# Weighing in column halves with turned blocks of inverses, and part of the keys on GpSimd

## The reference, cut to what matters

```python
# mixer A: 8 heads of 64; a 64-token chunk sees itself and the 8 chunks before, with a bias by distance
sc = jnp.einsum('bqhd,bkhd->bhqk', qc, kc) * scale + bias
p = jax.nn.softmax(sc, axis=-1)
o = jnp.einsum('bhqk,bkhd->bqhd', p, vc)
# mixer B: 8 query heads on 2 key heads, a chunk sees itself and the one before, with one sink per head
m = jnp.maximum(jnp.max(sc, axis=-1, keepdims=True), sink)
p = jnp.exp(sc - m)
p = p / (jnp.sum(p, axis=-1, keepdims=True) + jnp.exp(sink - m))
o = jnp.einsum('bnhgqk,bnkhd->bnqhgd', p, vb)
```

## Time and profile before

| | us |
|---|---|
| median of 3 runs | 2675.07 (2673.93 to 2676.16) |
| the profiled execution | 2678.14 |
| its span | 2676.2 |
| TensorE busy | 2631.9 (98%) |
| attention stage, first layer | 238.2 |
| attention stage, second layer | 237.5 |

### The profile page before, as it was taken

The page is one execution under the profiler, slowest core; times in us unless marked ns, Lnnn a source line. Parts: engine busy times, 40 slices in busy tenths (PEclk is TensorE's granted clock), DMA queues, the critical chain, the costliest instruction groups (busy, mean ns, idle before and its releaser), DMA issues. The chain is left out here.

```text
span 2676.2 us, 36725 instructions
## 1 busy us (share of the span) xinstructions
PE 2631.9 (98%) x12920; PEld 2208.2 (83%) x12920; DVE 1923.2 (72%) x3579; ACT 1159.0 (43%) x2429; POOL 252.6 (9%) x390
## 2 busy tenths in 40 slices
PE   8999999999999999999999999999999999999998
PEld 6888888888888888888878888888888888888886
DVE  8766667644787787767996666775448887776687
ACT  6222677732533333344542227775325333333444
POOL 0000311244100000000000011112440000000000
PEclk9999999999999999999999999999999999999999
DMA  4323433253222332385423243332531332234843
GB/s 147 122 104 115 155 102 111 75 183 115 87 99 103 114 118 84 106 269 176 153 99 122 99 144 123 119 97 88 188 120 61 114 110 88 103 114 136 267 124 126
DMA packets 185236, 333.21 MB, mean 125 GB/s; under 512 B 17248, under 2 KB 62688, under 8 KB 185056
## 3 DMA queue, kind: packets, MB, share of 16 engines
q1 hardware_dynamic: 176832, 307.67, 34.6%
q10 hardware_dynamic: 8224, 23.20, 2.6%
HBM read 237.09 MB, written 92.80 MB: 123 GB/s over the span
## 5 line engine op out<-in xcount | busy, mean ns | idle before, releaser
L1203 PE MATMUL ps<-op_hi,up_hi 128*128 128x512 f32 x1232 | 479.9, 390 | 2.5 <-DVE third_sum L2781 2.5
L1205 PE MATMUL ps<-op_hi,up_lo 128*128 128x512 f32 x1232 | 479.3, 389 | 0.0
L1204 PE MATMUL ps<-op_lo,up_hi 128*128 128x512 f32 x1232 | 479.3, 389 | 0.0
L1203 PE MATMUL ps<-in_hi,up_hi 128*128 128x512 f32 x728 | 286.9, 394 | 3.3 <-DVE up_lo L2279 2.1
L1205 PE MATMUL ps<-in_hi,up_lo 128*128 128x512 f32 x728 | 285.0, 392 | 0.0
L1204 PE MATMUL ps<-in_lo,up_hi 128*128 128x512 f32 x728 | 285.0, 392 | 0.0
L1878 ACT ACTIVATE up_hi<-up_raw 128x512 fp32r<-128x512 f32 x252 | 158.0, 630 | 276.9 <-PE ps L1205 271.1
L1203 PEld LDWEIGHTS ps<-op_hi,up_hi 128*128 128x128 f32 x1232 | 231.3, 188 | 51.1 <-issue 3.3
L1205 PEld LDWEIGHTS ps<-op_hi,up_lo 128*128 128x128 f32 x1232 | 231.3, 188 | 48.3
L1204 PEld LDWEIGHTS ps<-op_lo,up_hi 128*128 128x128 f32 x1232 | 231.3, 188 | 47.6
L1173 POOL CAST w_hi<-w_raw 128x256 fp32r<-128x256 f32 x192 | 85.3, 486 | 1757.7 <-DMA w_raw<-w_lin 1199.7
(11 more groups left out here) (266 smaller groups left out, 5406.8 us busy)
## 6 DMA issues: line engine op xcount, KB each, us to landing
up_raw<-w_gu SPq DMA_DIRECT2D x42, 1024.0 KB, 5.1
act_raw<-ff_saved SPq DMA_DIRECT2D x154, 256.0 KB, 2.7
w_quarter<-w_lin SPq DMA_DIRECT2D x52, 512.0 KB, 4.4
w_raw<-w_lin SPq DMA_DIRECT2D x48, 512.0 KB, 3.7
ff_saved<-ff_block SPq DMA_DIRECT2D x88, 256.0 KB, 2.0
ff_saved<-ff_mix SPq DMA_DIRECT2D x66, 256.0 KB, 2.1
gated<-gates_saved SPq DMA_DIRECT2D x32, 512.0 KB, 4.1
stage<-in_saved SPq DMA_DIRECT2D x48, 256.0 KB, 2.8
```

The source lines that it names most:

```text
L1203: pe.matmul(out, w1, x1, start=first, stop=False, skip_group_check=True)
L1204: pe.matmul(out, w1, x0, start=False, stop=False, skip_group_check=True)
L1205: return pe.matmul(out, w0, x1, start=False, stop=last, skip_group_check=True)
```

## The change

1. `weigh` takes two units (one pair) at once, in even steps. Stationary are now 64 columns of values (one head), moving are 128 columns of turned probabilities. Head 0 writes PSUM rows 0 to 63, head 1 rows 64 to 127, in turn for each block of keys. The built program gives these matmuls a tile of 128x64 of the array at column 0 or column 64; all other matmuls have the tile 128x128. The result comes out with head dimensions in rows, as `x_sb` wants it.
2. The inverses must then lie along the columns. `invert_pair` writes them spread over 2x64 columns (`wide`, 128x128 in place of 128x2), TensorE turns that block (`turn_wide`, where `turn_pair` was), ScalarE copies it to the place of the result in `x_sb` (`take_wide`), and `take_heads` multiplies the weighed values by it there.
3. In mixer B the two units of a pair are turned in the same step and copied out of PSUM by one instruction of 256 columns in place of two of 128. There are three buffers `probs_t`, and the probabilities of B use both halves of two of the `probs` buffers, so that six units have their own place.
4. The splitting of 14 of the 16 key halves of a layer goes from ScalarE and VectorE to GpSimd (`split_keys`), which also does its weight splits in single parts of 128x256 at fixed steps (`split_parts`) so that keys come between them.
5. `FILL_A` puts the gate products of A mostly into steps without weighing (26 in A0 and 8 in each later A phase, as before). `vb_odd` lies in two pieces, so one more DMA shifts values.

The core of the diff:

```diff
-FILL_A = ((3, 3, 3, 2, 2, 2, 2, 1, 1, 1, 1, 1, 1, 1, 1, 1), (1, 1, 1, 1, 1, 0, 1, 0, 1, 0, 0, 0, 1, 0, 0, 0))
+FILL_A = ((3, 3, 3, 3, 2, 3, 1, 2, 1, 1, 0, 1, 1, 1, 0, 1), (0, 1, 0, 2, 0, 1, 0, 1, 0, 1, 0, 1, 0, 1, 0, 0))
...
+            def split_keys(L, c):
+
+                kind, _, half = CONV[c]
+                e, cols = KEYS.index(kind), slice(half * HALF, (half + 1) * HALF)
+                made, value = plain_when(L, c)
+                pool.wait_ge(*staged_when(L, c))
+                pool.tensor_copy(ka_hi[e][:, cols], staged(c)).then_inc(made, 1)
+                pool.wait_ge(made, value - 1)
+                pool.tensor_tensor(ka_lo[e][:, cols], staged(c), ka_hi[e][:, cols], ALU.subtract).then_inc(made, 1)
...
             for L in range(DEPTH):
-                for t in range(TILES):
+                split(L, 0)
+                split(L, 1)
+                for s in range(UNITS):
+                    for c in conv_at(s, *KEYS):
+                        split_keys(L, c)
+                    for t, part in split_parts(s):
+                        split_part(L, t, part)
+                for t in range(GATE_TILES, TILES):
                     split(L, t)
...
-                pe.wait_ge(turned_ready, L * UNITS + u + 1)
-                n = L * (UNITS // 2) + u // 2
+                pe.wait_ge(turned_ready, L * TURN_GROUPS + groups_turned(u))
                 taken = n - 1 if mixer == "B" and u % PHASE > 1 else n
-                if e == 0 and taken > 0:
+                if taken > 0:
                     pe.wait_ge(head_free, taken)
                 for j in range(nb):
-                    mm = pe.matmul(o_ps(u)[:, e * HD:(e + 1) * HD], probs_t[u % 2][:, j * P:(j + 1) * P], values[j],
-                                   start=(j == 0), stop=(j == nb - 1))
+                    for e in range(2):
+                        rows = slice(e * HD, (e + 1) * HD)
+                        mm = pe.matmul(o_ps(u)[rows, :], blocks[j][:, rows], turns[e][:, j * P:(j + 1) * P],
+                                       start=(j == 0), stop=(j == nb - 1))
                 mm.then_inc(head_done, 1)
 
-            def turn_pair(L, u):
-
-                n = L * (UNITS // 2) + u // 2
-                pe.wait_ge(head_free, n + 1)
+            def turn_wide(L, s, u):
+
+                n = L * HEAD_PAIRS + u // 2
+                pe.wait_ge(inverse_ready, n + 1)
                 if n > 0:
-                    pe.wait_ge(pair_ready, n)
-                pe.transpose(p_ps, o_tok[:, n % 2, :], ident[:, :]).then_inc(pair_turned, 1)
+                    pe.wait_ge(wide_ready, n)
+                if values_before(s) > 0:
+                    pe.wait_ge(v_ready, L * VALUES + values_before(s))
+                pe.transpose(w_ps, wide[:, n % 2, :], ident[:, :]).then_inc(wide_turned, 1)
...
-                dve.reciprocal(st[:, :, 6:7], total).then_inc(inverse_ready, 1)
+                n = L * HEAD_PAIRS + u // 2
+                if n >= 2:
+                    dve.wait_ge(wide_turned, n - 1)
+                dve.reciprocal(wide[:, n % 2, :].rearrange("p (e d) -> p e d", e=2), total.to_broadcast([P, 2, HD])).then_inc(inverse_ready, 1)
...
-                inverse = stat[:, u % NSTAT - 1:u % NSTAT + 1, 6:7].to_broadcast([P, 2, HD])
-                dve.tensor_tensor(o_tok[:, n % 2, :].rearrange("p (e d) -> p e d", e=2),
-                                  o_ps(u).rearrange("p (e d) -> p e d", e=2), inverse, ALU.mult).then_inc(head_free, 1)
+                mixer, _, _, _ = unit(u)
+                n = L * HEAD_PAIRS + u // 2
+                dve.wait_ge(head_done, n + 1)
+                dve.wait_ge(wide_ready, n + 1)
+                src = o_ps(u) if mixer == "A" else o_ps(u).rearrange("p (h n) -> p h n", h=2)
+                dve.tensor_tensor(x_of(u), src, x_of(u), ALU.mult).then_inc(head_free, 1)
...
-                    if 2 <= s < UNITS + 2:
-                        turn(L, s - 2)
-                    if 3 <= s < UNITS + 3:
+                    u = s - 2
+                    if 0 <= u < UNITS:
+                        if unit(u)[0] == "A":
+                            turn(L, u)
+                        elif u % 2:
+                            turn(L, u - 1)
+                            turn(L, u)
+                    if s >= 4 and s % 2 == 0:
+                        turn_wide(L, s, s - 3)
                         weigh(L, s - 3)
```

More of the change, by code:

```diff
@@ L45 @@
 NPROBS = 3
+NTURNED = 3
+ODD_FIRST = 3
 NSTAT = 8
@@ L232, in fill_rate, with on_pool, plain_rank, split_parts @@
     return FILL_B[g] * (r + 1) // PHASE - FILL_B[g] * r // PHASE
+def on_pool(c):
+    return CONV[c][0] in KEYS and c >= CONV_AHEAD
+def plain_rank(c):
+    return sum(of_kind(other) == "plain" and on_pool(other) == on_pool(c) for other in range(c))
+def split_parts(s):
+    return [(t, part) for t in range(2, GATE_TILES) for part in range(2 * W_PARTS) if FILL_START[t - 1] + 1 + part // 2 == s]
 def fill_before(s):
@@ L1048, in shift_values @@
                 sp.wait_ge(v_ready, L * VALUES + V_PARTS * (rank(CONV.index(("vb", 0, half))) + 1))
[L1049 to L1052, removed]
+                low, high = slice(0, HD), slice(HD, P)
+                last = NBLK - 1 - ODD_FIRST
+                for rows, others, dst, src in (
+                        (low, high, vb_odd[0][low, :, :], 0), (low, high, vb_odd[1][low, 0:1, :], ODD_FIRST),
+                        (high, low, vb_odd[0][high, :, :], 1)) if half == 0 else (
+                        (low, high, vb_odd[1][low, 1:last, :], ODD_FIRST + 1), (high, low, vb_odd[1][high, :, :], ODD_FIRST + 1)):
+                    sp.dma_start(dst, vb[others, src:src + dst.shape[1], :]).then_inc(vb_shifted[half], 16)
             def load_rel(L, g):
@@ L1173, in split @@
                     pool.tensor_copy(w_hi[slot][:, k, :], w_raw[raw][:, k, :]).then_inc(hi_made, 1)
-                for part in range(W_PARTS):
-                    k = slice(part * KT // W_PARTS, (part + 1) * KT // W_PARTS)
-                    pool.wait_ge(hi_made, W_PARTS * number + part + 1)
+                else:
+                    pool.wait_ge(hi_made, W_PARTS * number + first + 1)
                     op = pool.tensor_tensor(w_lo[slot][:, k, :], w_raw[raw][:, k, :], w_hi[slot][:, k, :], ALU.subtract)
-                op.then_inc(tile_ready, 1)
@@ L1180, in _, with split @@
-            for L in range(DEPTH):
-                for t in range(TILES):
+                    if first == W_PARTS - 1:
+                        op.then_inc(tile_ready, 1)
+            def split(L, t):
+                for part in range(2 * W_PARTS):
+                    split_part(L, t, part)
[7 more added lines that the diff above has]
+                pool.tensor_tensor(ka_lo[e][:, cols], staged(c), ka_hi[e][:, cols], ALU.subtract).then_inc(made, 1)
@@ L1423, in attention @@
                 pe.wait_ge(in_taken, in_takes(L, IN_PAIRS - 1, 6))
-                for s in range(UNITS + 5):
+                for s in range(UNITS + 3):
                     if s < UNITS:
@@ L2541, in plain_parts @@
             def plain_parts(c):
-                return sum(2 if CONV[other][0] == "qa" else 1 for other in range(c) if of_kind(other) == "plain")
+                return sum(2 if CONV[other][0] == "qa" else 1 for other in range(c) if of_kind(other) == "plain" and not on_pool(other))
             def lower_half(L, c, parts=(0, 1)):
```

192 lines of the change are left out of this document (113 added, 79 removed).

## The result

The change made the kernel slower. The median of four runs went from 2674.5 us (2671.6 to 2676.2) to 2716.1 us (2712.9 to 2719.1), ratio 1.0157, 95% interval 1.0139 to 1.0174. The forecast of 2661 us had the wrong sign, and its range ended at 2698.

The account below looks back on a forecast made before the run. TensorE was taken to bound the attention stage, the others waiting for it. Passes -21, switches +8 and VectorE +6 gave -7 us a layer, -14 in both: 2661 us as the median of runs, range 2632 to 2698.

Parts of the forecast that it names:

- Passes in A, -21 a layer: Weighing on TensorE in A: overlapping halves save 5.2 us a phase, 21 us over four phases.
- Switches, 0.08 us: TensorE going between whole-array and half matmuls: 128 switches a layer at 0.08 us, +8 us after cover by waits.
- Rivals 1 and 3: First: switches free, VectorE keeps up, 2633 us, chance 0.16. Second: each switch drains the array, 0.27 us, 2705 us, 0.18.
- rival 4: Weighing on TensorE: the halves don't overlap, +16 us a layer, 2707 us, chance 0.14.
- Rival 2: TensorE's switches eat the gain: break-even at 0.13 us each; at 0.12, 2671 us, no change that can be told; chance 0.14.
- The inverse, 0.86 us: VectorE's inverse grows from 128x2 to 128x128: 0.86 us by slope, bounds 0.29 and 0.92, +44 us of work a layer.
- The charge of 6 us a layer: VectorE nearly full in the attention stage: 1.5 us each for A1 to A3, 0.4 each for four B phases.
- The turn of the inverses replaces that of the results one for one: TensorE's turns in the attention stage: same count, needing only an inverse made two steps earlier, so no cost.
- Keys on GpSimd, cost 0: 14 key halves a layer at 2.3 us each, mostly started 8 or more steps early, so covered by GpSimd's work.
- The forecast's own range: 2648 to 2670 us for the total, with switches from 0.04 to 0.11 us and VectorE's charge from 2 to 8.
- The signs that I had named: The forecast is wrong if B phases grow by more than 2 us, or if A1 stays above 31.
- theory D: From the experiments: in A the one score buffer's chain, scores, VectorE's row_max, next scores, holds the odd steps; no size given.

Follow-up runs that it names:

- serial kernel: The changed kernel with all passes of head 0 ahead of all passes of head 1 in a pair's weighing: 2738.1 us, ratio 1.0243.
- the chain cut as well: Changed kernel with short inverse, keys back, late turn; in A ScalarE copies only 128 columns of turned probabilities, leaving out computation: 2674.5 us, ratio 1.0003.
- undoing three parts: The changed kernel with a short inverse plus copy, keys back on ScalarE and VectorE, the turn of the inverses late: 2682.2 us, ratio 1.0037.

## Why the prediction was wrong

Point by point, by its own steps:

- **Passes in A, -21 a layer:** right. 20 passes in 1.25 us. The serial kernel shows what it hangs on.
- **Switches, 0.08 us:** right, 0.09. Rivals 1 and 3 fall, and with the overlap rival 4. That rivals 3 and 4 named 2705 and 2707 us, nearest to what came, is chance: neither of their mechanisms is there. Rival 2, the price eating the gain, is false too: the price is 128 x 0.09 = 11.5 us a layer and the gain 4 x (12.7 - 7.8 + 0.7) = 22.4.
- **The inverse, 0.86 us:** the slope was too low. (951 - 166) / 126 = 6.2 ns an element, where I took the mean of 6.0 and 5.25. The charge of 6 us a layer is not far from what undoing it gave (8 us in two layers, 4 a layer). VectorE's work in the stage is 195 us, 193 forecast.
- **"The turn of the inverses replaces that of the results one for one", cost 0:** this is the first step that failed. The count is right, the place is not. It stands ahead of weighing and gate steps, and it waits for all values copied so far (`values_before`). When ScalarE is late with them, 2 to 3 us of ready work stand behind the wait. Moving it back gave 22 of the 42 us, a part of it clock: the stretches at half clock went from 34 to 14 us. I had asked what the turn itself waits for, and only of its inverse; I had not asked what is queued behind it.
- **Keys on GpSimd, cost 0, because most start 8 steps early:** the second that failed. The keys themselves come in time mostly, and the 1.9 us each are below my 2.3. The exception is the last key of A0, 2.0 us in the first layer of the changed kernel. What came late beside it was what stands behind them: I named "weight parts and the next weight load on SyncE, needed only every 16 gate steps" and stopped there. Behind that load stand the loads of queries and keys, and behind those ScalarE's copies of values. Alone it costs 15 us, and 10 of them are this chain.
- **"The move of gate steps costs nothing":** borne out by itself (1.0048 against 1.0037). But the move of *weighing* into every second step, which I gave no price, is the third that failed. It took the cover from the chain turn, copy, next turn. With all else undone that is 8 us. That is a part only of why the -26 us of work never showed: with the chain cut as well, the kernel is just level with before, and 48 us of long waits remain in both layers (before 22), ahead of scores and of weighing in B.
- **The waits of the earlier trace rows as slack:** I let TensorE's gain count in full until VectorE or ScalarE is full, that is by sums over a phase. None was full: in A1 VectorE is busy 27.9 of 35.5 us and ScalarE 23.9. The limit was latency between engines, with one buffer each in the loops above.
- **The clock:** the prediction has no term for it. In the kernel before the stage ran at 1.00. The longer waits brought 34 us at half clock.
- **The forecast's own range** doesn't follow from its bounds: -21 + 3 + 2 and -21 + 12 + 8 a layer give 2643 to 2673 us, not 2648 to 2670. What was measured lies outside either.

The signs that I had named did decide it: A1 stayed above 31 (35.5), and B0 and B2 grew by 6 us each. Of the four rivals none was this one; all were about prices on TensorE.

Of the 42 us, undoing three parts gives 32 and cutting ScalarE's copy 8 more. Not won back are the 26 us saved on TensorE; they are lost to waits that no run takes away. By the trace of the changed kernel, the 26 us and the 42 together are 68: the waits above 0.15 us grew by 31 us in a layer, 62 in both, and the other 6 lie in shorter waits and in the slow stretches. How much of the 62 is matmuls at half clock isn't parted. Left open are the joined turning of pairs in B, with 12 us of waits ahead of its weighing, and theory D: a second place in PSUM for turned probabilities or for the scores of A would test them.

## What to carry to other kernels

When an instruction takes another's place one for one, ask what it waits for and what stands behind it on its engine, and follow the answer through the queues until it ends on the engine that bounds the kernel; a load queue that also waits for a helper engine is part of that path. Gathering work in every second step to save on it also takes away the cover of the short loops in the other steps, so that an engine's sum over a phase says little where a buffer has one place. Column halves paid here only when they were issued in turn. And a wait can cost more than its length, when the clock behind it falls.

## What the runs showed of the hardware

- Two column halves issued in turn start 0.054 us apart in the mean; in runs of one half, twenty take 1.95 us in place of 1.25. So half-width passes of 128 columns by themselves are little faster than the whole passes of 64 columns before (2.1 us for twenty).
- Going from whole to half and back adds 0.09 us each way to the normal 0.11.
- A wait of 3.5 us on TensorE was followed by about 4 us at a granted clock of 0.57, and the one ahead of 339.27 us in the changed kernel, 2.3 us long, by 10 us at 0.50 (the row of 339.10). Not every such wait is. In the run with the weight parts ahead of the keys, behind the wait of 2.35 us ahead of 300.13, the clock stayed at 1.00; behind the one of 3.0 us at the same place in the second layer it was 0.63 over 4 us.

- VectorE's inverse costs 6.2 ns an element at 128x128 (951 ns), 3.5 times its copy of the same shape (270 ns). The Trainium skill (VectorE: DVE Perf Modes, First, the fixed hardware budget) gives a repeat count of 8 for it. Read as 8 cycles an element, that was 1.2 us by my estimate; the trace shows less.
- GpSimd took 1.9 us for a key half of 128x512 (0.61 the cast, 1.28 the subtraction) where ScalarE and VectorE take 0.62 and 0.78.
